# The attention of a two-layer block in units of two heads, with the value product turned round

## The reference, cut to what matters

```python
def second_block(x, ...):
    for layer in range(2):
        h = rms_norm_2(x, g_mix[layer]); qkv = h @ w_in[layer]
        o_a = differential_attention(qa, ka, va, ...)   # 4 heads: a = p[:,:,0] - lam * p[:,:,1]; o = a @ v; rms_norm_2(o)
        o_b = moba_attention(qb, kb, vb, positions)     # 4 heads: with 512 tokens a plain causal softmax
        o_c = dilated_attention(qc, kc, vc, positions)  # 8 heads: softmax under a banded, dilated mask
        x = x + jnp.concatenate([o_a, o_b, o_c], axis=-1) @ w_out[layer]
        x = x + conv_gated_mlp(rms_norm_2(x, g_ffn[layer]), ...)
    return rms_norm_2(x, g_final)
```

## Time and profile before

| | us |
|---|---|
| median of 3 runs (lowest, highest) | 2205.19 (2205.01, 2206.89) |
| the profiled execution | 2204.52 |
| its span, first to last instruction | 2202.7 |
| PE, DVE, ACT, POOL busy in the span | 2150.4, 1501.5, 946.7, 1197.0 |
| attention of layer 0, first score to first product with w_out | 1024.71 to 1129.99 |
| attention of layer 1 | 1674.85 to 1780.13 |

### The profile page before, as it was taken

The page is one execution under the profiler, slowest core; times in us unless marked ns, Lnnn a source line. Parts: engine busy times, 40 slices in busy tenths (PEclk is TensorE's granted clock), DMA queues, the critical chain, the costliest instruction groups (busy, mean ns, idle before and its releaser), DMA issues.

```text
span 2202.7 us, 33160 instructions
## 1 busy us (share of the span) xinstructions
PE 2150.4 (98%) x12377; PEld 1837.3 (83%) x12377; DVE 1501.5 (68%) x2234; ACT 946.7 (43%) x1891; POOL 1197.0 (54%) x594
## 2 busy tenths in 40 slices
PE   6999999999999999999999999999999999999997
PEld 4787888787899988897887898888897887888886
DVE  6844877654666692897737677677996728777676
ACT  3264663112465600645744555412555725555312
POOL 4766404765576677654026545577653037544675
PEclk9999999999999999999999999999999999999998
DMA  8322103422232343232002232322221012223221
GB/s 324 152 77 96 58 21 115 172 96 77 77 114 99 115 158 115 78 114 77 1 20 79 94 115 77 115 96 95 96 97 58 1 39 85 92 93 115 96 96 58
DMA packets 32776, 206.78 MB, mean 94 GB/s; under 512 B 4080, under 2 KB 4336, under 8 KB 11632
## 3 DMA queue, kind: packets, MB, share of 16 engines
q1 hardware_dynamic: 32192, 200.27, 24.8%
q10 hardware_dynamic: 432, 4.46, 0.5%
HBM read 202.61 MB, written 2.10 MB: 93 GB/s over the span
## 4 chain that ended last, share of the span: by engine, by line
PE 87%; DVE 6%; issue 1%; DMA 1%; ACT 1%; DVEq 1%; POOL 1%; POOLq 1%; SPq 0%; ACTq 0%
PE PS L1126 18%; PE PS L1128 18%; PE PS L1127 18%; PE PS L1605 5%; PE PS L1617 5%; PE PS L1381 3%; PE PS L1382 3%; PE PS L1383 3%; PE PS L1631 3%; PE PS L1457 2%; PE PS L1459 2%; PE PS L1458 2%; PE PS L1256 1%; PE PS L1259 1%; PE PS L1258 1%
## 5 line engine op out<-in xcount | busy, mean ns | idle before, releaser
L665 POOL TENSOR_TENSOR w_hi<-raw,zero_c 128x512 fp32r<-128x512 f32 (+1 forms) x135 | 281.6, 2104 | 536.0 <-PE PS L1128 534.5
L669 POOL TENSOR_TENSOR w_lo<-raw,w_hi 128x512 fp32r<-128x512 f32 (+1 forms) x135 | 366.2, 2731 | 5.8
L1126 PE MATMUL PS<-b_hi,w_hi 128*128 128x512 f32 x512 | 203.1, 397 | 0.9 <-POOL w_lo L888 0.9
L1127 PE MATMUL PS<-b_lo,w_hi 128*128 128x512 f32 x512 | 203.0, 396 | 0.0
L1128 PE MATMUL PS<-b_hi,w_lo 128*128 128x512 f32 x512 | 203.0, 396 | 0.0
L3346 DVE TENSOR_TENSOR b_lo<-a_all,b_hi 128x512 fp32r<-128x512 f32 x44 | 162.5, 3733 | 49.3 <-ACT b_hi L2491 49.3
L1126 PE MATMUL PS<-f_hi,w_hi 128*128 128x512 f32 x448 | 177.6, 397 | 0.7 <-DVE f_lo L2648 0.7
L1128 PE MATMUL PS<-f_hi,w_lo 128*128 128x512 f32 x448 | 177.6, 396 | 0.0
L1127 PE MATMUL PS<-f_lo,w_hi 128*128 128x512 f32 x448 | 177.6, 396 | 0.0
L688 POOL TENSOR_TENSOR w_lo<-raw,w_hi 128x512 fp32r<-128x512 f32 x48 | 71.0, 1478 | 90.5 <-ACT w_hi L2483 90.5
L1126 PEld LDWEIGHTS PS<-b_hi,w_hi 128*128 128x128 f32 x512 | 96.4, 188 | 24.6 <-POOL w_lo L888 1.1
(11 more groups left out here) (586 smaller groups left out, 6858.8 us busy)
## 6 DMA issues: line engine op xcount, KB each, us to landing
raw<-slabs_dram SPq DMA_DIRECT2D x161, 1024.0 KB, 4.8
aux<-ada_dram SPq DMA_DIRECT2D x18, 512.0 KB, 5.4
ada_first<-ada_dram SPq DMA_DIRECT2D x11, 512.0 KB, 14.0
cmpw<-cmpw_dram ACTq DMA_DIRECT2D x2, 2048.0 KB, 11.5
ada_late<-ada_dram SPq DMA_DIRECT2D x8, 512.0 KB, 3.2
ada_last<-ada_dram SPq DMA_DIRECT2D x8, 512.0 KB, 5.6
xT<-xT_dram SPq DMA_DIRECT2D x1, 2048.0 KB, 9.0
out_dram<-t SPq DMA_DIRECT2D x4, 512.0 KB, 3.2
```

What stands on the lines that cost most here:

```text
L665: high = nc.gpsimd.tensor_tensor(w_hi[:, slot, c], raw[:, slot, c], zero[:, 0:c.stop - c.start], ALU.add)
L669: low = nc.gpsimd.tensor_tensor(w_lo[:, slot, c], raw[:, slot, c], w_hi[:, slot, c].bitcast(f32), ALU.subtract)
L1126: nc.tensor.matmul(out, a_hi_, b_hi_, start=start, stop=False)
L1127: nc.tensor.matmul(out, a_hi_, b_lo_, start=False, stop=False)
```

## The change

A layer's attention is now a list of 45 units. A unit holds two score tiles: the same query block of two plain or two dilated heads ("pair", 24 of them), or the two maps of one differential head ("diff", 16); four units hold two transposes each of later heads' operands ("turn") and one holds those of the two differential output blocks ("out"). In step t PE issues the scores of unit t, the values of unit t-5 and the transposes of unit t-3.

For a pair the values are stationary (64 columns for each head) and the transposed probabilities move (128 columns); the two heads write partitions 0 to 63 and 64 to 127 of one bank. The output comes out transposed, so six of the eight output blocks need no transposes, only the split into high and low. The division by the row sum can't be made there any more: DVE takes one reciprocal of two sums, and POOL multiplies the two tiles of probabilities by it before they are transposed. A diff unit still has its probabilities stationary. The joins are made tile by tile. One tile of each pair is copied by ACT and one by DVE. POOL splits the two slabs of w_out in pieces of 512 columns, one piece (a high and a low instruction) behind each pair from the second to the ninth. The blocks of code for SyncE and GpSimd are moved behind the definitions and are otherwise the same; some semaphores are merged. The first four banks of the product with w_out stand among the last five steps.

```diff
-        ring_2 = at("ring_2", 81920, [P, 9, SEQ])
-        ring_x = at("ring_x", 32768, [P, 4, SEQ])
-        ring_y = at("ring_y", 116736, [P, 3, SEQ])
+        ring_2 = at("ring_2", 81920, [P, 16, SEQ])
...
-        DIFF_SQ, DIFF_SUM, DIFF_ROOT, DIFF_SCALE = 58, 60, 62, 64
-        O2_TURNS = [(56, 4, 3), (59, 5, 7), (63, 0, 10), (67, 6, 8), (70, 7, 8), (73, 1, 12), (80, 2, 14)]
...
+        LAG_T, LAG_V, LAG_OUT = 3, 5, 6
+        W_MASKED, W_PROBS, W_TURNED = 4, 8, 4
...
+        def two_units():
+            units, groups = [], [Group(n, b) for n, b in enumerate((4, None, 5, None, 0, 1, 2, 3))]
+            singles = {1: (8, 9), 2: (10, 11), 4: (12, 13), 5: (14, 15)}
+            for i in (0, 1):
+                for n, j in enumerate((3, 0, 2, 1)):
+                    units.append(Unit("pair", plain_jobs[2 * i:2 * i + 2], j, groups[2 * i]))
+                    for half in (0, 1):
+                        units.append(Unit("diff", diff_jobs[2 * i + half:2 * i + half + 1], j, groups[2 * i + 1], half))
+                    if 4 * i + n in singles:
+                        units.append(Unit("turn", items=singles[4 * i + n]))
+            for i in range(4):
+                for j in (3, 0, 2, 1):
+                    units.append(Unit("pair", dilated_jobs[2 * i:2 * i + 2], j, groups[4 + i]))
+            units.insert(DIFF_AT + 7, Unit("out", items=(6, 7)))
+            return Weave(units)
+        DILATED_AT = 28
+        DIFF_AT = DILATED_AT - 1 + LAG_OUT
+        DIFF_SQ, DIFF_SUM, DIFF_ROOT, DIFF_SCALE = (DIFF_AT + n for n in (1, 2, 3, 4))
...
+            def pieces_of(n):
+                slot, nth = n % 2, n // 2
...
+                for a in range(0, SLAB, PIECE):
+                    c = slice(a, a + PIECE)
+                    high = nc.gpsimd.tensor_tensor(w_hi[:, slot, c], raw[:, slot, c], zero[:, 0:PIECE], ALU.add)
+                    if a + PIECE == SLAB:
+                        high.then_inc(hi_done, 1)
+                    pool.drain()
+                    low = nc.gpsimd.tensor_tensor(w_lo[:, slot, c], raw[:, slot, c], w_hi[:, slot, c].bitcast(f32),
+                                                  ALU.subtract)
...
+                for u in plan.units:
+                    if u.kind != "pair":
+                        continue
+                    pool.wait_ge(inverted, plan.pairs * layer + u.pair + 1)
+                    inv = pair_inv(u)
+                    for c in (0, 1):
+                        p = w_probs(u.score + c, 128 * u.nb)
+                        last = nc.gpsimd.tensor_scalar(p, p, inv[:, c:c + 1], None, ALU.mult)
+                    last.then_inc(scaled_probs, 1)
+                    if u.pair > 0:
+                        next(pieces, None)
...
+                            q, k = u.operands(c)
+                            nc.tensor.matmul(out[:, 0:128 * u.nb], query_tile(q, u.j),
+                                             k[:, 128 * u.lo:128 * (u.lo + u.nb)], start=True, stop=True
+                                             ).then_inc(scores_ready, 1)
...
+                    for c in (0, 1) if u.kind == "pair" else (1,):
+                        v = u.tile + (c if u.kind == "pair" else 0)
+                        if u.kind == "diff":
+                            pe.wait_ge(combined, at_.pair + u.join + 1)
+                        elif c == 0:
+                            pe.wait_ge(scaled_probs, at_.scaled + u.pair + 1)
+                        if v >= PT_BANKS:
+                            copied_before(v - PT_BANKS)
+                        for b in range(u.nb):
+                            last = nc.tensor.transpose(PS[:, S_BANKS + v % PT_BANKS, 128 * b:128 * b + 128],
+                                                       w_probs(u.score + c, 512)[:, 128 * b:128 * b + 128], ident)
+                        last.then_inc(probsT_ready, 1)
...
+                def values(u):
+                    pe.wait_ge(copied_act, at_.acopies + u.on_act)
+                    if u.kind == "pair":
+                        pe.wait_ge(copied_dve, at_.dcopies + u.on_dve)
+                    if u.first and u.group.index >= O_BANKS:
+                        pe.wait_ge(out_used, at_.map + plan.released[u.group.index - O_BANKS])
+                    bank = u.group.bank
+                    for b in range(u.nb):
+                        if u.kind == "pair":
+                            for c in (0, 1):
+                                last = nc.tensor.matmul(PS[64 * c:64 * c + 64, bank, 128 * u.j:128 * u.j + 128],
+                                                        u.jobs[c]["v"](u.lo + b),
+                                                        w_turned(u.tile + c, 512)[:, 128 * b:128 * b + 128],
+                                                        start=b == 0, stop=b == u.nb - 1)
+                        else:
+                            a = 256 * u.half + 64 * u.j
+                            last = nc.tensor.matmul(PS[:, bank, a:a + 64],
+                                                    w_turned(u.tile, 512)[:, 128 * b:128 * b + 128],
+                                                    u.jobs[0]["v"](u.lo + b), start=b == 0, stop=b == u.nb - 1)
+                    last.then_inc(pv_done, 1)
...
+                for t in range(len(plan.units) + LAG_V):
+                    u = plan.at(t)
+                    if u is not None:
+                        front(u)
+                    else:
+                        tail(t - len(plan.units))
+                    for lag, part in ((LAG_V, values), (LAG_T, turns)):
+                        u = plan.at(t - lag)
+                        if u is not None and u.jobs:
+                            part(u)
...
-                attend(two_jobs, (ring_2, ring_x, ring_y), s_banks=3, banks_ready=two_operands, also=o2_also, fill=FILL_2)
...
+                def tail(n):
+                    if n == 0:
+                        pe.wait_ge(slab_split, at_.slab + 1)
+                        for i in (0, 1):
+                            pe.wait_ge(block_low, low0 + plan.low[i])
+                    if n < 4:
+                        first_banks((plan.units[-2].bank, plan.units[-2].bank + 1,
+                                     plan.units[-1].bank, plan.units[-1].bank + 1)[n])
...
+                    A(w_turned(v, 128 * u.nb), PS[:, S_BANKS + v % PT_BANKS, 0:128 * u.nb], ACT.Copy
+                      ).then_inc(copied_act, 1)
...
+                    if u is not None and u.last and u.kind == "pair":
+                        act.wait_ge(pv_done, p0 + u.value)
+                        A(o_high(u.group.block), PS[:, u.group.bank, :], ACT.Copy).then_inc(block_high, 1)
...
+                def weigh(u):
+                    dve.wait_ge(probs_ready, g0 + u.score + 2)
+                    a = sum_at(u, 0)
+                    if u.kind == "pair":
+                        V.reciprocal(pair_inv(u), SUMS[:, a:a + 2]).then_inc(inverted, 1)
+                        return
+                    b = sum_at(u, 1)
+                    r = ratio[:, u.join % 4:u.join % 4 + 1]
+                    one, two = (w_probs(u.score + c, 128 * u.nb) for c in (0, 1))
+                    then(V.reciprocal(r, SUMS[:, b:b + 1]))
+                    then(V.scalar_tensor_tensor(out=r, in0=r, scalar=lam_c, in1=SUMS[:, a:a + 1], op0=ALU.mult,
+                                                op1=ALU.mult))
+                    V.scalar_tensor_tensor(out=two, in0=two, scalar=r, in1=one, op0=ALU.mult, op1=ALU.add
+                                           ).then_inc(combined, 1)
...
+                    V.tensor_copy(w_turned(v, 128 * u.nb), PS[:, S_BANKS + v % PT_BANKS, 0:128 * u.nb]
+                                  ).then_inc(copied_dve, 1)
...
+                    if g.block is not None:
+                        block_rest(g.block, g.bank)
+                        dve.drain().then_inc(out_used, 1)
+                        return
...
+                for t in range(len(plan.units) + LAG_OUT):
+                    u = plan.at(t)
+                    if u is not None:
+                        front(u)
+                    u = plan.at(t - 1)
+                    if u is not None and u.jobs:
+                        weigh(u)
...
```

More of the change, by code:

```diff
@@ L1643, in _, with woven @@
+            def woven(plan):
+                at_.tile += plan.scores
+                at_.value += plan.tiles
+                at_.pvs += plan.values
+                at_.pair += plan.joins
+                at_.scaled += plan.pairs
+                at_.map += plan.groups
+                at_.acopies += plan.on_act
+                at_.dcopies += plan.on_dve
             meet()
```

735 lines of the change are left out of this document (450 added, 285 removed).

## The result

| | before | after |
|---|---|---|
| median of 20 runs, us | 2204.15 | 2208.16 |
| lowest, highest | 2202.53, 2207.03 | 2205.37, 2210.60 |
| ratio (95% interval) | | 1.0016 (1.0009 to 1.0023) |
| a layer's attention, layer 0 and 1 | 105.3, 105.3 | 106.3, 107.5 |
| of it up to the first dilated score | 53.5, 53.5 | 56.9, 57.2 |

A forecast was written before the change was run, and what follows sets the result against it. PE was taken to bound the kernel before; after, DVE the first part. 59.0 + 42.4 = 101.4 us a layer against 105.3, so -7.8 for two layers and a median of 2197.4; range (8 in 10) 2184 to 2210.

The forecast's parts named there:

- PE's side: PE's work in a layer's attention: 102.4 us, less 2.6 transposes and 12.9 pair values, plus 8.2 switching, gives 95.1.
- rival D: Pair values: the two array halves don't run at once, so values gain nothing and switches stay; 2216 us, chance 0.04.
- The round trip: PE switching into and out of half-array mode around each pair's values: 0.33 or 0.34 us, 24 a layer, 8.2 us.
- a dilated part over 46: Sign to check: a layer's dilated part, forecast at 42 us, lasting over 46 would make the switches' price wrong.
- The lock between POOL and DVE: First part: joins wait for POOL's w_out pieces, one hit of 1.2 us behind each of 7, 8.4 us a layer.
- The first part's 59.0: Attention up to the first dilated score: DVE sets the pace, 50.6 us of work plus 8.4 of waits for POOL.
- PE's 41.0 with 1.4 of waits: Dilated part: PE's work of 41.0 us plus waits as before gives 42.4 us, against 51.9 before.
- Hidden, at those prices: POOL's scaling of pairs is ready before PE's transposes three units later: slack 2.2 us, gone above 2.1 per 512-column tile.
- POOL's price: POOL scaling one 512-column tile in place: 1.04 us taken from a product by a broadcast factor, upper bound 1.27.
- my chain of 7.0: From a pair's score through mask, exponential, reciprocal, a POOL piece and two scalings: about 7.0 us, against 9.2 available.
- Rival B: No change: scaling late in the first part, 2 us a layer or more, and switches at 0.48; 2203 to 2207, chance 0.17.
- Rival C: Slower: the POOL and DVE lock delays joins, masks and PE; 2229 us at the upper bound, chance 0.12.

The follow-up runs named there:

- best version: Changed kernel with ACT's copy first, ACT scaling one tile per pair, DVE's norm spread, w_out pieces of 256 columns behind pairs 7 to 22: 2196.1 us.
- h5: The best version with ACT's copy back behind the two exponentials and the norm of its step: 2206.4 us.
- h8: The changed kernel with only the w_out pieces made 256 columns wide and put behind pairs 7 to 22: 2222.4 us.
- e4: The changed kernel with the first tile of each pair scaled by ACT, POOL keeping the second: 2205.4 us.
- g2: The changed kernel with ACT's copy of a turned tile ahead of the two exponentials of its step: 2210.8 us.
- h4: The changed kernel with DVE's norm of the differential heads behind the copy and spread over later steps: 2207.4 us.

## Why the prediction was wrong

PE's side held. A pair's row costs 0.054 as forecast, which leaves rival D with nothing. The round trip was taken as 0.34 and is 0.29, so PE's work is 94.8 - 24 x 0.05 = 93.6 a layer. The six blocks that come out transposed need no turn. POOL's new operation showed no load of its code: POOL had been idle for 26.7 us when the first two scalings came, and they took 3.11 together, no more than later ones. One of my signs was wrong: a dilated part over 46 was to show a wrong price of the switches. It lasted 49.5 with that price a little lower than forecast, since waits lengthen the part as well.

The lock between POOL and DVE is there, as in the earlier trace rows, but its size was off. I had 8.4 us in the first part. The 15 small products recorded in that stretch take 5.3 where 15 x 0.22 = 3.3 would do, and the joins themselves 10.0 against 8.3 at the lengths of before: 3.7. Leaving out the pieces gave back 2.2 a layer. The first part's 59.0 against a measured 56.9 and 57.2 was thus near by luck: DVE was busy for 48.6 of them and not the bound.

The step that failed is the term of the waits: "PE's 41.0 with 1.4 of waits" in the dilated part, and with it "Hidden, at those prices" for the scaling. In all I had 101.4 - 94.8 = 6.6 us a layer that aren't PE's work. It is 106.3 - 93.6 = 12.7 in layer 0 and 13.9 in layer 1, of which the profile shows 10.6 and 10.2 as waits. Within this:

- POOL's price. The nearest row, 1.04 for 512 columns, was too low; it is 1.62, above my upper bound of 1.27. And the slack of 9.2 was worked out from the steps of the first part (3.1 us); a dilated step is 2.6. With 1.62 my chain of 7.0 becomes 8.2, and two tiles of 512 are late there. That is 3.7 us of PE's waits in layer 0, 2.0 of them for the first pair, which belong to the filling of the lags. The run with thin scaling shows that by itself it decides nothing.
- The copies: 6.1 us of waits in layer 0, where the kernel before had 2.1 and I had carried over 1.4. (Of the 6.1, the 1.6 at 1080.4 are DVE's join as much.) They are shown by the wait rows, and by the place of ACT's copy in the last version, under that version's conditions (10.3 us). I had counted how busy DVE and ACT would be, and not when within a step an in-order queue comes to the one instruction that PE needs.
- The clock, for which I had no term, as the rows of before stood at 1.00: in layer 1 the rest that no wait explains is 13.9 - 10.2 = 3.7 instead of 12.7 - 10.6 = 2.1, and this is the stretch at half clock from 1687.4, behind a wait of 2.0. The same wait in layer 0 has no such stretch behind it.

The sum of that term was short by 6.1 and 7.3 us a layer, which is the difference between -3.9 and the measured +1.1 and +2.2, after PE's 1.2. Rival B came nearest to the time (2203 to 2207) and named a part of the reason, scaling that is late; its other part, dearer switches, is out. Rival C had the right sign and the wrong mechanism.

Why did single edits do little or harm? The runs show that the waits replace each other: without scaling the copies are late, with ACT's copy early DVE's is late, with that one moved POOL's tile is late. An edit alone removed or shortened the wait that it aimed at, and another took its place. Where the two edits of ACT's order came out slower, and not only the same, the profiles show the lower clock behind a long wait; how much of it is in the medians is open. Nor did any run take apart how much of the best version's 12.1 us is each edit's; h5 and h8 show that one edit's worth depends on the others.

## What to carry to other kernels

When a change makes a unit of work larger, look for the buffers that didn't grow with it, and for what now stands ahead of the instruction that frees them: here one unit fills both banks, and two exponentials stand ahead of the copy instead of one. With little slack, price a hand-over by what stands ahead of it in its engine's queue at that moment, not by the engine's busy share. And when several in-order engines feed one, try their reorderings together: the edits of the last versions gave between -2.8 and +14.3 us where one was tried alone (e4, g2, h4, h8), and together they turned +4.0 us against the kernel before into -8.5. Read the granted clock beside the waits: a long wait of PE can cost more than its own length.

## What the runs showed of the hardware

Multiplying a tile in place by one value of each partition took POOL 1.62 us for 512 columns and 0.61 for 128, and still 0.31 for 8, while the same tile took ACT 0.71, copied with a scale. Column tiles that alternate between two halves ran at 0.054 us for a row of 128 columns each, with 0.29 for going there and back. Behind waits of PE of about 2 to 3 us, or from within them, the granted clock was at its lower level for 3.4 to 6.8 us in several profiles, and not behind each such wait. In one kernel, with the same waits in both layers, 3.4 us of it made a layer 1.5 us longer; in another, four score rows of 256 columns spanned 1.91 us instead of 1.03.
